# Sparse attention begun between the products of its query projection

## The reference, cut to what matters

```python
hn = rms_norm_2(h, mix_norm_pre[l])
proj = hn @ w_in[l]
rq, rk, rv, rg, aq, ak, av, iq, ik, iw = split_columns(proj)
...
ret_out = retention(rq, rk, rv, rg)
aq = apply_rope(aq.reshape(B, S, DSA_HEADS, HEAD_DIM), cos_h, sin_h)
...
att_out = dsa_attention(aq, ak, av, iq, ik, iw)
mixed = jnp.concatenate([ret_out, att_out], axis=-1) @ w_out[l]
...
def dsa_attention(q, k, v, qi, ki, wi):
    ...
        _, sel = lax.top_k(iscore, k_sel)
        valid = sel <= t[None, :, None]
        ...
        logits = jnp.where(valid[:, None], logits, -1e30)
        p = jax.nn.softmax(logits, axis=-1).astype(v.dtype)
        return jnp.einsum('bhtk,btkd->bhtd', p, v_g)
```

## Time and profile before

| | |
|---|---|
| runs before, us | 3180.6 median of 3 (3179.82 to 3183.84) |
| the profiled execution | 3181.32 us, of which the span is 3179.2 us |
| TensorE busy | 2939.3 us, 92% of the span |
| VectorE, ScalarE, GpSimd busy | 1315.5, 1045.8, 1012.6 us |
| mean granted clock of TensorE | 0.952 |
| items of `A_` | about 2020 to 2096 us |
| `sparse_phase` | 2098 to 2303 us |

### The profile page before, as it was taken

The page is one execution under the profiler, slowest core; times in us unless marked ns, Lnnn a source line. Parts: engine busy times, 40 slices in busy tenths (PEclk is TensorE's granted clock), DMA queues, the critical chain, the costliest instruction groups (busy, mean ns, idle before and its releaser), DMA issues. The chain is left out here.

```text
span 3179.2 us, 37512 instructions
## 1 busy us (share of the span) xinstructions
PE 2939.3 (92%) x14048; PEld 2431.6 (76%) x14048; DVE 1315.5 (41%) x2088; ACT 1045.8 (33%) x1863; POOL 1012.6 (32%) x700
## 2 busy tenths in 40 slices
PE   2999999999999999999997987879999999998998
PEld 2878887887788888787885766758777888886877
DVE  6646557222700000114658876543445322323143
ACT  3215545002510000024545564334443222222243
POOL 2011122334523333245521132420063333332454
PEclk9999999999999999999999998857999999998999
DMA  5531112323311111133411130000061111112342
GB/s 182 192 100 34 28 40 61 92 67 119 133 40 46 46 52 47 39 120 126 140 47 40 47 106 27 21 0 1 1 205 47 53 46 53 46 46 73 96 146 90
DMA packets 196107, 230.17 MB, mean 72 GB/s; under 512 B 11657, under 2 KB 140809, under 8 KB 195977
## 3 DMA queue, kind: packets, MB, share of 16 engines
q1 hardware_dynamic: 195976, 228.44, 22.5%
HBM read 203.24 MB, written 25.17 MB: 72 GB/s over the span
## 5 line engine op out<-in xcount | busy, mean ns | idle before, releaser
L133 PE MATMUL psum<-sb_h_hi,sb_w_hi 128*128 128x512 f32 x1792 | 709.4, 396 | 13.9 <-POOL sb_w_lo L928 8.7
L135 PE MATMUL psum<-sb_h_hi,sb_w_lo 128*128 128x512 f32 x1792 | 702.3, 392 | 0.0
L134 PE MATMUL psum<-sb_h_lo,sb_w_hi 128*128 128x512 f32 x1792 | 701.7, 392 | 0.0
L1539 POOL TENSOR_TENSOR sb_out_lo<-sb_out_raw,sb_out_hi 128x512 fp32r<-128x512 f32 (+1 forms) x180 | 323.5, 1804 | 396.0 <-ACT sb_out_hi L1529 395.9
L133 PEld LDWEIGHTS psum<-sb_h_hi,sb_w_hi 128*128 128x128 f32 x1792 | 339.1, 189 | 86.5 <-POOL sb_w_lo L928 9.9
L133 PE MATMUL psum<-sb_out_hi,sb_a_hi 128*128 128x512 f32 x960 | 383.3, 399 | 19.5 <-DVE sb_a_lo L1534 10.6
L135 PEld LDWEIGHTS psum<-sb_h_hi,sb_w_lo 128*128 128x128 f32 x1792 | 338.8, 189 | 71.9
L134 PEld LDWEIGHTS psum<-sb_h_lo,sb_w_hi 128*128 128x128 f32 x1792 | 339.2, 189 | 68.4
L926 POOL TENSOR_SCALAR sb_w_hi<-sb_w_raw 128x1024 fp32r<-128x1024 f32 x97 | 102.4, 1055 | 895.3 <-PE psum L135 615.2
L134 PE MATMUL psum<-sb_out_lo,sb_a_hi 128*128 128x512 f32 x960 | 379.0, 395 | 0.0
L135 PE MATMUL psum<-sb_out_hi,sb_a_lo 128*128 128x512 f32 x960 | 378.8, 395 | 0.0
(11 more groups left out here) (392 smaller groups left out, 4389.9 us busy)
## 6 DMA issues: line engine op xcount, KB each, us to landing
sb_w_raw<-in_w_up SPq DMA_DIRECT2D x44, 512.0 KB, 3.8
sb_late_w<-in_w_ada SPq DMA_DIRECT2D x32, 512.0 KB, 4.8
sb_w_raw<-in_w_in SPq DMA_DIRECT2D x56, 256.0 KB, 3.0
sb_w_raw<-in_w_ffn_gate SPq DMA_DIRECT2D x22, 512.0 KB, 3.8
sb_w_raw<-in_w_ffn_up SPq DMA_DIRECT2D x22, 512.0 KB, 3.8
sb_out_raw<-in_w_ffn_down SPq DMA_DIRECT2D x22, 512.0 KB, 3.5
sb_out_raw<-in_w_ffn_down SPq DMA_DIRECT2D x44, 256.0 KB, 3.0
sb_out_raw<-in_w_down SPq DMA_DIRECT2D x22, 512.0 KB, 3.5
```

The costliest lines, as they stand in the source:

```text
L133: nc.tensor.matmul(out, stationary.hi, moving.hi, start=start, stop=False)
L134: nc.tensor.matmul(out, stationary.hi, moving.lo, start=False, stop=False)
L135: return nc.tensor.matmul(out, stationary.lo, moving.hi, start=False, stop=stop)
L1539: self.nc.gpsimd.tensor_tensor(w.lo, raw, w.hi.bitcast(F32), ALU.subtract).then_inc(self.w_lo, 1)
```

## The change

The sparse stage becomes a class, `Sparse`, whose methods give each engine its part of one unit, and `spread_phase` calls them. Fifteen units (0 to 14) are placed in the items 4 to 7 of `A_`: the table `EARLY` names those for each item. On TensorE a unit stands ahead of every second step (`begin`): unit 0 ahead of k = 3 and units 1, 2 ahead of 5 and 7 in item 4, and in the others four units ahead of 1, 3, 5 and 7. The scores of units 0 and 1 are computed ahead of k = 1 of item 4. On VectorE and ScalarE the units stand between the pieces of rotation, choice and copies. Units 15 to 63 follow the last item in one stream without loops; parts 6 and 7 are turned after units 16 and 20. There is no barrier between the two stages.

The units' buffers take the place of the first half of the activations (`h`), which tiles 4 to 7 do not read. The items of `A_` use banks 0 and 1 alone, the query parts banks 2 and 3. Scores of tiles 0 to 3 (one bank wide) take bank 4 or 5, later ones the pairs 0, 1 and 2, 3. Probabilities of tiles 0 to 3 are turned into bank 7. The queries are read from `q_tiles` directly, without GpSimd's copy. The rows of a tile are turned some units after its end (`ROWS_AFTER`), out of one of four buffers. The scan of `choose` becomes a function of its own, `add_up`.

```diff
+class Sparse:
...
+    def score_bank(self, u):
+        return 4 + u % 2 if u < 4 * RH else 2 * (u % 2)
...
+    def turn(self, pe, u):
+        t = u // RH
+        pe.wait_ge(self.exp_done, u + 1)
+        if u:
+            pe.wait_ge(self.t_out_act, u)
...
+    def values(self, pe, u):
+        t, head = u // RH, u % RH
+        pe.wait_ge(self.t_out_act, u + 1)
+        if t >= 4:
+            pe.wait_ge(self.t_out_dve, u - 4 * RH + 1)
+        if head == 0 and t:
+            pe.wait_ge(self.o_ready, t)
...
+    def head(self, pe, u):
+        self.turn(pe, u)
+        if u + 2 < self.many:
+            self.scores(pe, u + 2)
+        self.values(pe, u)
...
+    def rows_of(self, dve, chain, u):
+        if u >= 4 * RH:
+            self.turned_low(dve, u)
+        if u + 2 < self.many:
+            self.maximum(dve, chain, u + 2)
+        if u % RH == RH - 1:
+            self.scaled(dve, chain, u // RH)
...
+    def probs_of(self, act, u):
+        self.turned_high(act, u)
+        if u + 2 < self.many:
+            self.exponent(act, u + 2)
...
+EARLY = {4: ((0,), (1, 2)), 5: ((3, 4), (5, 6)), 6: ((7, 8), (9, 10)), 7: ((11, 12), (13, 14))}
+ROWS_AFTER = {23: 0, 25: 1, 27: 2, 32: 3, 40: 4, 48: 5, 56: 6, 63: 7}
...
+        bank = lambda n: n % 3 if n < A_ * TB else n % 2
...
+                def attending(n, t):
+                    first, second = EARLY[t] if t in EARLY else ((), ())
+                    begin = {5 - 2 * len(first) + 2 * m: u for m, u in enumerate(first)}
+                    begin.update({5 + 2 * m: u for m, u in enumerate(second)})
+                    for k in range(KD):
+                        if k == 5:
+                            turn_parts(t - 2)
+                        if t == 4 and k == 1:
+                            pe.wait_ge(q_out, 1)
...
+                            att.scores(pe, 0)
+                            att.scores(pe, 1)
+                        if k in begin:
+                            unit(begin[k])
+                        steps(n, k, k + 1)
...
-                        steps(n, 0, 5)
                         if t >= 2:
-                            turn_parts(t - 2)
-                        steps(n, 5, KD)
+                            attending(n, t)
+                        else:
+                            steps(n, 0, KD)
...
-                turn_parts(TB - 2)
-                turn_parts(TB - 1)
+                for u in range(15, TB * RH):
+                    unit(u)
+                    if u in (16, 20):
+                        turn_parts(TB - 2 + (u == 20))
...
+                    if u in ROWS_AFTER:
+                        att.turn_rows(pe, ROWS_AFTER[u])
...
+                    for u in first[0:1]:
+                        att.rows_of(dve, chain, u)
+                    if j in range(NP_):
+                        top.add_up(dve, chain, j)
+                    for u in first[1:]:
+                        att.rows_of(dve, chain, u)
                     if j in range(NP_):
                         top.choose(dve, chain, j)
+                    for u in second[0:1]:
+                        att.rows_of(dve, chain, u)
                     if j + 1 in range(NP_):
                         top.above_at(dve, chain, j + 1)
+                    for u in second[1:]:
+                        att.rows_of(dve, chain, u)
...
+                    if n - A_ * TB == 4:
+                        att.exponent(act, 0)
+                        att.exponent(act, 1)
+                    for u in first:
+                        att.probs_of(act, u)
+                    if 0 <= n - 2 - A_ * TB < TB - 2:
                         parts_out(n - 2 - A_ * TB)
-                    if 0 <= n - 1 - A_ * TB < TB:
+                    if 0 <= n - 1 - A_ * TB < TB - 1:
                         parts_high(n - 1 - A_ * TB)
+                    for u in second[0:1]:
+                        att.probs_of(act, u)
                     j = n - A_ * TB - 1
                     if j in range(NP_):
                         top.sum_above(act, j)
+                    for u in second[1:]:
+                        att.probs_of(act, u)
+                for u in range(15, TB * RH):
+                    att.probs_of(act, u)
+                    if u == 16:
+                        parts_out(TB - 2)
+                        parts_high(TB - 1)
+                    if u == 20:
+                        parts_out(TB - 1)
...
-def sparse_phase(core, q_tiles, k_parts, av, bias, attT, cst):
```

More of the change, by code:

```diff
@@ L2598, in steps @@
                             pe.wait_ge(lo_done, c * KD + k + 1)
-                        done = multiply(nc, core.ps[:, n % 3, :], h.tile(k, t), w[:, k], k == 0, k == KD - 1)
+                        done = multiply(nc, core.ps[:, bank(n), :], h.tile(k, t), w[:, k], k == 0, k == KD - 1)
                         if t == TB - 1:
@@ L2613, in turn_parts, with unit @@
                     pe.wait_ge(q_lo, t + 1)
[L2614 to L2618, removed]
+                    if t:
+                        pe.wait_ge(q_out, t)
                     else:
-                        pe.wait_ge(ret.s_out, TB)
+                        pe.wait_ge(turn_out, len(turns))
                     for q in range(RH):
-                        last = nc.tensor.transpose(core.ps[:, 4 + 2 * (t % 2) + q // 4, q % 4 * P:(q % 4 + 1) * P],
+                        last = nc.tensor.transpose(core.ps[:, 2 + q // 4, q % 4 * P:(q % 4 + 1) * P],
                                                    q_rows[:, q, :, :].bitcast(F32), cst["ident"])
                     last.then_inc(q_turned, 1)
+                def attending(n, t):
[7 more added lines that the diff above has]
+                            pe.wait_ge(q_out, 1)
+                            pe.wait_ge(ret.s_out, TB)
+                            pe.wait_ge(ret.o_read, TB)
+                            pe.wait_ge(ret.sq_done, TB)
+                            pe.wait_ge(ret.st_ready, TB + 1)
+                            att.scores(pe, 0)
[3 more added lines that the diff above has]
+                        steps(n, k, k + 1)
+                def unit(u):
+                    if (u + 2) % RH == 0 and u + 2 < TB * RH:
+                        pe.wait_ge(q_out, (u + 2) // RH + 1)
+                    if u + 2 == 4 * RH:
+                        pe.wait_ge(dve_read, roped[N])
+                        pe.wait_ge(q_out, TB)
+                    att.head(pe, u)
                 def turn_free(what):
@@ L2769, in parts_out @@
                     act.wait_ge(q_turned, t + 1)
-                    src = core.ps[:, 4 + 2 * (t % 2):6 + 2 * (t % 2), :].rearrange("p b (h q) -> p (b h) q", q=P)
+                    src = core.ps[:, 2:4, :].rearrange("p b (h q) -> p (b h) q", q=P)
                     nc.scalar.activation(q_tiles[t][:, :, :], src, ACT.Copy).then_inc(q_out, 1)
                 highs(0)
-                for n in range(N + 2):
-                    c, t = items[n] if n < N else (None, None)
+                for n in range(N):
+                    c, t = items[n]
                     if c == G_:
@@ L2973, in small_layouts @@
+                    for u in second[1:]:
+                        att.probs_of(act, u)
+                for u in range(15, TB * RH):
+                    att.probs_of(act, u)
[4 more added lines that the diff above has]
+                        parts_out(TB - 1)
+                    if u in ROWS_AFTER:
+                        att.rows_out(act, ROWS_AFTER[u])
 def small_layouts():
```

252 lines of the change are left out of this document (105 added, 147 removed).

## The result

The changed kernel took 3146.55 us (median of 4 executions, 3139.09 to 3153.76), the kernel before 3181.26 us beside it: ratio 0.9889, 95% interval 0.9873 to 0.9905. The profiled execution took 3149.47 us, its span is 3147.6 us, 31.6 less than before. The forecast was 3169: the direction was right, the gain is 34.7 us and not 12.1. Of all executions here one, of the kernel with rows turned at once, was slow (6743 us), and it is left out of that kernel's time.

What follows compares the result with a forecast made beforehand. Bounds: the projection's end where TensorE waits, the sparse stage's first four tiles at half clock, and tile ends. Terms -5.9 + 2.0 - 4.8 - 3.4 = -12.1 us took 3180.6 to 3168.5, say 3169 us; own range 3160 to 3178, with rivals 3146 to 3184.

Steps and rivals of the forecast that it cites:

- the head start: Up to the values of unit 17: starting early units among the products leaves 5.9 us saved (2132.4 instead of 2138.28).
- The ring: Items 4 to 7: engines pass work round to the next rotation; TensorE joins, taking 26 us more by item 6's rotation.
- the walk: Step-by-step timing of items 4 to 7 from the profile's durations, with rotations at about 2070, 2088.5, 2108 and 2124 us.
- I cost both at nothing: Sparse stage: removing GpSimd's query copies and the loops saves nothing, since TensorE is busy all the time.
- I take half clock for both tiles, as before: Tiles 2 and 3: TensorE stays at 1.2 GHz, so no saving from the clock there.
- Rival 1: Tiles 2 and 3 at full clock, as no barrier but dense products stand in front: 3154 us, chance 0.19.
- its term of 14.7: Full clock in tiles 2 and 3: units 18 to 23 save 0.85 each, tile 3 saves 8 x 1.2.
- the 2.2 for ends: Ends of tiles 2 and 3 no longer hold TensorE: 1.1 us saved at each.
- Tile ends: Ends of tiles 2 to 6 no longer hold TensorE, -4.8 us; two later clock dips there vanish, -3.4 us.
- The transposes of part 7, +2.0: Query part 7's transposes, formerly ahead of the sparse stage, now stand in it: 2.0 us more.
- Rival 3: Half clock holds on through tile 4, 12.4 us more: 3193 us, chance 0.07.
- rival 2: Half clock through items 5 to 7, +12.1 us together: 3181 us, no change, chance 0.12.

Runs made afterwards that it cites:

- the kernel with rows turned at once: Changed kernel with output rows of tiles 3 to 6 turned right behind each tile's last unit, not one unit later: 3157.12 us, median of three.
- the new stage in the old place: Changed kernel with all 64 units behind the last product and query parts 6 and 7 turned ahead of the first unit: 3141.75 us.
- the kernel with the pause in units 15 to 31: Changed kernel with the values of units 15 to 31 each inside a TensorE loop of one round: 3146.22 us.

## Why the prediction was wrong in size

The sum had 12.1 us, the length fell by 35.3. Of the 23.2 us between them, 4.3 lie in the head start, 13.9 in tiles 2 and 3, 4.8 in tiles 4 to 7 and 0.2 behind.

**The ring, right, slightly long.** TensorE did join it by the path that the walk named, idled from 2054.7 to 2061.0 us (forecast 2048.6 to some 2055, plus the 5.7 us of delay ahead of it), and the rotations took 66.7 us for four items where the walk had 72.6. The clock, back some 6 us after the first long wait, was back in 3 to 4 us after the next three, not in 5.5, and 10 us after the one before unit 16. Head start: 10.2 us, not 5.9. But the experiments show whose it is: with no early unit at all the values of unit 17 start 74.5 us after item 3's rotation (2131.75 - 2057.28), with the early units 76.4. The ring and the early units cancel, slightly to the bad. The head start comes from the stage's new form: the same stretch is 86.6 us before, 84.6 with all loops written out, 79.9 without the copies too, and 76.6 with the new stage in the old place. So the forecast had its head start from a source that gave none, and that the direction came out right is luck in this part.

**The step that failed first: "The queries' copies on GpSimd and the loops go too; I cost both at nothing, since a TensorE that is busy all the time shows no room for a saving there."** Writing out the loops is worth 14.6 to 18.1 us of length, the copies then 9.6; writing out TensorE's loops alone was worth 23.8 to 27.3, so such sizes do not add up term by term. A TensorE that is busy all the time at half clock does show room: what it is busy with could run at twice the rate. I took the busy share as proof that nothing else held the stage.

**The second: "So I take half clock for both tiles, as before."** Rival 1, at 0.19, came true in its outcome there, with full clock from unit 19 on: tiles 2 and 3 from unit 17 on took 35.4 us instead of 49.5, 14.1 less, where its term of 14.7 with the 2.2 for ends and the 2.0 back for transposes makes 14.9. Neither of its reasons is borne out. Full clock there needs no dense products in front (the stage in the old place has it as well), and the barrier may stay: the old stage with TensorE's loops alone written out had it back at 2133 us. A wait ahead of unit 17 did not forbid it. The Trainium skill (TensorE: Matmul & The Clock Gate, Part 1: The HAM clock gate), which I set aside on the trace's 20 busy us at 0.50, pointed to the right outcome in the changed kernel, with 1.00 from 2160 to 2180 us (TensorE busy 18.61 of 20 us); in the kernel before, the trace still goes against it.

**Tile ends, too small.** The forecast had 2.6 for the ends of tiles 4 to 6 and 3.4 for two dips, 6.0 in all; tiles 4 to 7 are 10.8 shorter, of which turning the rows late is 5.4, dips included. Of the rest, 5.4, the loops and copies are some 3.9: without them and with the old ends, tiles 4 to 7 take 109.8 us, with them 113.8. The two numbers overlap, since one of before's two dips is gone there as well; with TensorE's loops alone written out and no dip at all, the four tiles took 109.3 us. No dip is left at any tile end, as forecast.

**The transposes of part 7, +2.0:** they cost 1.5 us in the stream, since units 20 and 21 start 3.26 us apart around them, and 1.80 apart in the kernel that turns them ahead:

```profile
2141.18 0.88 PE L2566 MATMUL psum<-sb_av,sb_probs_T 128*128 128x64 f32 x6 [0.27 <-ACT sb_probs_T L2630]
2141.90 1.04 PE L2766 MATMUL psum<-sb_consts,sb_q_rows 128*128 128x128 f32 x8
...
2144.44 0.88 PE L2566 MATMUL psum<-sb_av,sb_probs_T 128*128 128x64 f32 x6 [0.82 <-ACT sb_probs_T L2630]
```

Turned ahead they cost a wait instead, and both parts together save nothing that can be told from scatter (1.8 us).

Rival 3's 3193 us adds its 12.4 to the time before, 3180.6, which is where rival 2 ends. On the forecast's 3168.5 it gives 3181, no change, so it stands only on top of rival 2.

What stays open is how far each part of the old stage delays the clock. Counted from the rotation of item 7 it came back after 99 and 109 us in two traces of before, 67 without the other engines' loops, 61 without any, 41 without TensorE's alone, 27 without loops and copies (and then down for another 10), 36 with the new stage behind the products, and 53 when that was given pauses. That the loops prolong the half clock, and that register work and its pauses on TensorE alone can, is shown, by the traces and by the mean clocks of all executions; that writing out all loops helped less than writing out TensorE's alone is not explained, and with one trace of each kernel it may be chance.

## What to carry to other kernels

A stretch in which an engine is busy all the time at half clock is not a floor: price it at both levels, and take away what the units wait for (loops, a copy through a slow engine) before moving work about. In this kernel, work put between dense products paid only once no long wait inside it went round through the engine that the products feed; look at what stands ahead of its copy on each in-order engine. And when a change does two things, price the one that its name leaves out: here the rewritten stage was all of the gain, and the early start gained nothing (1.0 to 3.4 us longer) until the orders around it were turned round.

## What the runs showed of the hardware

A stage of short fp32 products stayed at 1.2 GHz for 102 us in one trace of before, up to 2187 us, with TensorE busy 81 of the last 87 us (20.00 of 20 us in the earlier trace rows), and for 113 us in the other. In four kernels that do the same products without TensorE's loops, or with one of 0.05 us a unit, it stayed there for 34 to 44 us. Where all loops were written out and the copies stayed it was 65 us, so the distance of units on TensorE alone does not settle it. Among the 512-column products of the changed kernel the clock fell around waits of 3.05, 3.51 and 3.69 us and was back in 3 to 4 us; in the same items of the kernel with the pause in units 15 to 31 it was back 5 to 6 us after two such waits. How much half clock a program gets varies from one execution to the next: the kernel before took 3153 us once and 3192 us another time, and its mean granted clock was 0.963 and 0.947 there.
